# Stick-breaking sums on the scores' own PSUM bank, and attention scores over 64 partitions, in a two-block fp32 transformer kernel

## What is computed

```python
q = heads(proj[..., :MIX_WIDTH]); k = ...; v = ...
q = jnp.concatenate([partial_rope(q[:, :n_rot], pos), q[:, n_rot:]], axis=1)   # heads A and B turned
k = jnp.concatenate([partial_rope(k[:, :n_rot], pos), k[:, n_rot:]], axis=1)

def stick_breaking_attention(q, k, v):
    z = jnp.einsum('bhqd,bhkd->bhqk', q, k) * Dh ** -0.5
    log_1m = jnp.where(causal, jax.nn.log_sigmoid(-z), 0.0)          # causal is strict: key < query
    suffix = lax.cumsum(log_1m, axis=3, reverse=True) - log_1m
    a = jnp.where(causal, jnp.exp(jax.nn.log_sigmoid(z) + suffix), 0.0)
    return jnp.einsum('bhqk,bhkd->bhqd', a, v)
```

## Time and profile before

| | us |
|---|---|
| median of 3 runs | 2152.02 |
| lowest, highest | 2151.99, 2154.15 |
| the profiled execution | 2152.88 |
| its span in the profile | 2151.1 |

### The profile page before, as it was taken

One profiled execution on the slowest core, in us unless ns is written; L12 is line 12 of the kernel. 1 busy time (PEld: TensorE's weight loads), 2 busy tenths in 40 slices (PEclk: granted clock), 3 DMA queues, 4 the chain that ended last, 5 costly groups with the idle time before them and its releaser, 6 DMA issues.

```text
span 2151.1 us, 36602 instructions
## 1 busy us (share of the span) xinstructions
PE 2051.2 (95%) x15510; PEld 1966.5 (91%) x15510; DVE 930.2 (43%) x1761; ACT 917.4 (43%) x1393; POOL 1332.5 (62%) x612
## 2 busy tenths in 40 slices
PE   7999997999989999889999999999999999999998
PEld 4999996899989998769998999989999999988998
DVE  4554776561455477754124422144233432134223
ACT  2443454334444335434444354514544345514543
POOL 1778660477967786217887765505896765405885
PEclk8999998999989999999999999999999999999999
DMA  9997550785689775227555543335554543335552
GB/s 326 357 332 253 186 161 20 254 289 176 195 275 349 244 245 167 79 84 250 177 162 170 170 146 116 103 126 166 186 194 134 192 143 113 118 118 168 185 196 79
DMA packets 356787, 398.18 MB, mean 185 GB/s; under 512 B 8984, under 2 KB 318992, under 8 KB 356624
## 3 DMA queue, kind: packets, MB, share of 16 engines
q1 hardware_dynamic: 356464, 395.65, 55.5%
q10 hardware_dynamic: 160, 0.20, 0.0%
HBM read 394.77 MB, written 1.05 MB: 184 GB/s over the span
## 4 chain that ended last, share of the span: by engine, by line
PE 90%; DVE 5%; ACT 3%; SPq 1%; issue 1%; DMA 1%; DVEq 0%; ACTq 0%
PE bank L706 73%; PE bank L783 5%; PE bank L1108 3%; PE bank L938 1%; PE bank L805 1%; PE bank L900 1%; PE bank L1072 1%; SPq L534 1%; DVE arena L1641 1%; ACT arena L1270 1%; PE bank L697 1%; PE bank L999 1%; DVE arena L1685 1%; DMA arena<-in_ada_w 1%; PE bank L939 1%
## 5 line engine op out<-in xcount | busy, mean ns | idle before, releaser
L672 POOL TENSOR_TENSOR w_lo<-ring,w_hi 128x1024 fp32r<-128x1024 f32 (+2 forms) x608 | 1332.3, 2217 | 798.7 <-ACT w_hi L1169 798.1
L706 PE MATMUL bank<-hn,w_hi 128*128 128x256 f32 x2912 | 848.4, 291 | 26.4 <-DVE hn_lo L1578 15.8
L706 PE MATMUL bank<-hn_lo,w_hi 128*128 128x256 f32 x2912 | 832.4, 286 | 0.0
L706 PE MATMUL bank<-hn,w_lo 128*128 128x256 f32 x2912 | 832.1, 286 | 0.0
L1169 ACT ACTIVATE w_hi<-ring 128x1024 fp32r<-128x1024 f32 (+2 forms) x608 | 576.4, 975 | 485.6 <-PE bank L706 356.8
L706 PEld LDWEIGHTS bank<-hn,w_hi 128*128 128x128 f32 x2912 | 567.6, 195 | 36.7 <-issue 34.6
L706 PEld LDWEIGHTS bank<-hn_lo,w_hi 128*128 128x128 f32 x2912 | 567.8, 195 | 4.5 <-issue 3.8
L706 PEld LDWEIGHTS bank<-hn,w_lo 128*128 128x128 f32 x2912 | 567.3, 195 | 0.0
L706 PE MATMUL bank<-gated,w_hi 128*128 128x256 f32 x1408 | 249.7, 280 | 0.0
L706 PEld LDWEIGHTS bank<-gated,w_hi 128*128 128x128 f32 x1408 | 215.0, 187 | 0.0
L706 PE MATMUL bank<-gated,w_lo 128*128 128x256 f32 x704 | 196.4, 279 | 0.0
(11 more groups left out here) (188 smaller groups left out, 2130.1 us busy)
## 6 DMA issues: line engine op xcount, KB each, us to landing
ring<-in_ffn_w_in SPq DMA_DIRECT2D x88, 1024.0 KB, 6.1
ring<-in_w_in SPq DMA_DIRECT2D x72, 1024.0 KB, 5.1
arena<-in_ada_w SPq DMA_DIRECT2D x35, 2048.0 KB, 10.3
ring<-in_w_up SPq DMA_DIRECT2D x32, 1024.0 KB, 5.4
ring<-in_w_down SPq DMA_DIRECT2D x32, 1024.0 KB, 5.0
ring<-in_ffn_w_out SPq DMA_DIRECT2D x32, 768.0 KB, 4.4
ring<-in_ffn_w_out SPq DMA_DIRECT2D x32, 640.0 KB, 4.0
ring<-in_w_in SPq DMA_DIRECT2D x16, 512.0 KB, 3.6
```

The costliest lines, as they stand in the source:

```text
L672: pool.tensor_tensor(w_lo[:, q, ks], ring[:, r, k0:k0 + n], w_hi[:, q, ks], ALU.subtract) \
L706: last = mm(out, a, b, start=start and i == 0, stop=stop and i == 2)
```

## The change

1. `turned` of a stick head no longer computes the scores a second time. Its three products with sp accumulate onto the bank that `stick_scores` wrote, and that bank stays taken until ScalarE has copied it out (`copied`). Stick heads get four banks in turn (2, 3, 4, 5, kind "stick banks") instead of two and two.
2. `q2` has 12 pair tiles instead of 24 masked tiles. `scores` takes the 64 partitions of the head of both `q2` and `k2`, so that the score products of block two have 64 contraction rows: rows 0 to 63 for even heads, 64 to 127 for odd ones.
3. The rotary units of q and k go one way now: VectorE multiplies by cos and by the scale in one instruction, and no longer writes two masked copies for q; the half unit of k copies with a scale. ScalarE scales q as it copies out of the bank, and unit 5 is one ScalarE instruction instead of two.

```diff
--- before.py
+++ after.py
@@ -337,8 +337,8 @@
 def place_heads(heads):
 
-    n = {"two banks": 0, "four banks": 0, "tp": 0, "pb": 0, "ps": 0}
-    banks = {"two banks": (2, 3), "four banks": (2, 3, 0, 1), "pb": (4, 5)}
+    n = {"two banks": 0, "four banks": 0, "stick banks": 0, "tp": 0, "pb": 0, "ps": 0}
+    banks = {"two banks": (2, 3), "four banks": (2, 3, 0, 1), "stick banks": (2, 3, 4, 5), "pb": (4, 5)}
     last = {}
 
     def take(kind, size, frees):
@@ -354,9 +354,8 @@
     for u, h in enumerate(heads):
         h.u, h.pair = u, u // 2
         if h.kind == "stick":
-            h.sb = [take("two banks", 2, f"sp {h.name}")]
+            h.sb = [take("stick banks", 4, f"copied {h.name} 0")]
             h.tp = [take("tp", SLOTS, f"sp {h.name}"), take("tp", SLOTS, f"arg {h.name}")]
-            h.pb = [take("pb", 2, f"copied {h.name} 0")]
             h.ps = [take("ps", SLOTS, f"out {h.name}")]
         else:
             turned = 1 if h.kind == "diff" else len(h.maps)
@@ -452,7 +451,7 @@
         rows_n2 = view(8192 + 1536, P)
         rows_c = view(8192 + 1664, P)
 
-        q2 = view(0, 24, S)
+        q2 = view(0, 12, S)
         k2 = view(6144, 12, S)
         v2 = view(9216, 2, MIXW2)
         gates = view(12288, 24, S)
@@ -873,13 +872,13 @@
                     if of:
                         ada_reduce(*of)
 
-            def stick_scores(b, q, k, qi, ki, stop):
-
-
-                mm(b[:, 0:256], k[:, ki, 0:P], q[:, qi, :], start=True, stop=False)
-                mm(b[:, 256:384], k[:, ki, P:S], q[:, qi, P:S], start=False, stop=False)
+            def stick_scores(b, q, k):
+
+
+                mm(b[:, 0:256], k[:, 0:P], q, start=True, stop=False, skip_group_check=True)
+                mm(b[:, 256:384], k[:, P:S], q[:, P:S], start=False, stop=False, skip_group_check=True)
                 for c0 in (0, 256):
-                    last = mm(b[:, c0:c0 + P], ident_r[:], unseen[:], start=False, stop=stop and c0 > 0)
+                    last = mm(b[:, c0:c0 + P], ident_r[:], unseen[:], start=False, stop=c0 > 0, skip_group_check=True)
                 return last
 
             def scores(hd, q, k, maps=(0, 1)):
@@ -890,9 +889,15 @@
                     if free:
                         pe.wait_ge(done_by(free), eng.at(free))
                     b = bank[:, sbk]
+                    if hd.kind != "diff" and hd.kind != "fox":
+                        half = slice(64 * (qi % 2), 64 * (qi % 2) + 64)
+                        qh, kh = q[half, qi // 2], k[half, ki]
                     if hd.kind == "stick":
 
-                        last = stick_scores(b, q, k, qi, ki, True)
+                        last = stick_scores(b, qh, kh)
+                    elif hd.kind == "soft":
+                        mm(b[:, 0:P], qh[:, 0:P], kh[:, 0:P], start=True, stop=True)
+                        last = mm(b[:, P:SCW], qh[:, P:S], kh, start=True, stop=True)
                     else:
                         fox = hd.kind == "fox"
                         for c0, c1, n in ((0, P, P), (P, SCW, S)):
@@ -906,15 +911,11 @@
             def turned(hd, q, k, tile):
                 if hd.kind == "stick":
 
-                    (qi, ki, _, _), (pb, free) = hd.maps[0], hd.pb[0]
-                    if free:
-                        pe.wait_ge(done_by(free), eng.at(free))
-                    b, sp_ = bank[:, pb], tile[:, hd.tp[1][0], :]
-                    stick_scores(b, q, k, qi, ki, False)
+                    b, sp_ = bank[:, hd.sb[0][0]], tile[:, hd.tp[1][0], :]
                     pe.wait_ge(vector_done, eng.at(f"sp {hd.name}"))
-                    mm(b[:, 0:256], tab("neg_suffix"), sp_[:, 0:256], start=False, stop=False)
-                    mm(b[:, 128:256], tab("neg_ones"), sp_[:, 256:384], start=False, stop=False)
-                    mm(b[:, 256:384], tab("neg_suffix"), sp_[:, 256:384], start=False, stop=True) \
+                    mm(b[:, 0:256], tab("neg_suffix"), sp_[:, 0:256], start=False, stop=False, skip_group_check=True)
+                    mm(b[:, 128:256], tab("neg_ones"), sp_[:, 256:384], start=False, stop=False, skip_group_check=True)
+                    mm(b[:, 256:384], tab("neg_suffix"), sp_[:, 256:384], start=False, stop=True, skip_group_check=True) \
                         .then_inc(tensor_done, eng.step(f"arg {hd.name}"))
                     return
                 pe.wait_ge(vector_done, eng.at(f"scaled {hd.name}"))
@@ -1276,7 +1277,7 @@
                     act.wait_ge(tensor_done, eng.at(f"arg {hd.name}"))
                     if hd.ps[0][1]:
                         act.wait_ge(tensor_done, eng.at(hd.ps[0][1]))
-                    f(tt[:, hd.ps[0][0]], bank[:, hd.pb[0][0], 0:SCW], ACT.Exp) \
+                    f(tt[:, hd.ps[0][0]], bank[:, hd.sb[0][0], 0:SCW], ACT.Exp) \
                         .then_inc(scalar_done, eng.step(f"copied {hd.name} 0"))
                     return
                 for m in range(len(hd.pb)):
@@ -1409,13 +1410,12 @@
                     if i in ROTARY:
                         if p >= 2:
                             act.wait_ge(tensor_done, eng.at(f"rotary {ROTARY[p - 2]}"))
-                        f(raw[:, p % 2], b, ACT.Copy).then_inc(scalar_done, eng.step(f"z2 out {i}"))
+                        f(raw[:, p % 2], b, ACT.Identity, scale=0.125 if i < 6 else 1.0) \
+                            .then_inc(scalar_done, eng.step(f"z2 out {i}"))
                         return
                     b = b.rearrange("p (t s) -> p t s", t=2)
                     if i == 5:
-                        for a in range(2):
-                            f(q2[:, 4 * i:4 * i + 4, :].rearrange("p (t a) s -> p t a s", a=2)[:, :, a], b, ACT.Identity,
-                              scale=tab("in64_eighth", 1, a)).then_inc(scalar_done, eng.step(f"z2 out {i}" if a else None))
+                        f(q2[:, 10:12, :], b, ACT.Identity, scale=0.125).then_inc(scalar_done, eng.step(f"z2 out {i}"))
                         return
                     if i == 11:
                         dst = k2[:, 10:12, :]
@@ -1899,26 +1899,16 @@
                     rot = bank[:, 5 + n % 2].rearrange("p (c s) -> p c s", c=2)
                     half = i % 6 == 4
                     t = 1 if half else 2
-                    tt(by_cos[:, 0:t], src[:, 0:t], cosb[:, 0:t], ALU.mult) \
+                    dst, k0, scale = (q2, 2 * i, 0.125) if i < 6 else (k2, 2 * (i - 6), 1.0)
+                    stt(by_cos[:, 0:t], src[:, 0:t], scale, cosb[:, 0:t], ALU.mult, ALU.mult) \
                         .then_inc(vector_done, eng.step(None if half else f"by cos {i}"))
                     tt(rot[:, 0:t], rot[:, 0:t], sinb[:, 0:t], ALU.mult).then_inc(vector_done, eng.step())
+                    if half:
+                        ts(dst[:, k0 + 1, :], src[:, 1], scale, None, ALU.mult) \
+                            .then_inc(vector_done, eng.step(f"by cos {i}"))
                     dve.wait_ge(vector_done, eng.at())
-                    if i < 6:
-                        dst = q2[:, 4 * i:4 * i + 4, :].rearrange("p (t a) s -> p t a s", a=2)
-                        tt(rot[:, 0:t], rot[:, 0:t], by_cos[:, 0:t], ALU.add).then_inc(vector_done, eng.step())
-                        for m in range(2 if half else 0):
-                            ts(dst[:, 1, m], src[:, 1], tab("in64_eighth", 1, m), None, ALU.mult) \
-                                .then_inc(vector_done, eng.step(f"by cos {i}" if m else None))
-                        dve.wait_ge(vector_done, eng.at())
-                        for m in range(2):
-                            ts(dst[:, 0:t, m], rot[:, 0:t], tab("in64_eighth", 1, m), None, ALU.mult) \
-                                .then_inc(vector_done, eng.step(f"rotated {i}" if m else None))
-                    else:
-                        k0 = 2 * (i - 6)
-                        if half:
-                            dve.tensor_copy(k2[:, k0 + 1, :], src[:, 1]).then_inc(vector_done, eng.step(f"by cos {i}"))
-                        tt(k2[:, k0:k0 + t, :], rot[:, 0:t], by_cos[:, 0:t], ALU.add) \
-                            .then_inc(vector_done, eng.step(f"rotated {i}"))
+                    tt(dst[:, k0:k0 + t, :], rot[:, 0:t], by_cos[:, 0:t], ALU.add) \
+                        .then_inc(vector_done, eng.step(f"rotated {i}"))
                     dve.wait_ge(vector_done, eng.at())
                 attention(HEADS_TWO, tile2, lambda hd: o2[:, hd.out_tile, :], lambda i: None)
                 for i in range(4):
```

## The result

Over nine runs of each, the kernel after takes 2157.02 us (2156.12 to 2158.99) where the kernel before takes 2152.21 us (2151.27 to 2154.15). The ratio is 1.0022, with an interval of 1.0012 to 1.0032. So it is slower by 4.8 us; the forecast was 0.2 us less, and the result lies 0.02 us above the upper end of the range. The profiled execution after took 2156.4 us, with a span of 2154.5 against 2151.1 before.

The account below looks back on a forecast made before the run. TensorE, busy for 95% of the span, was taken to bound the kernel. Part 1's -10.4 and part 2's +10.2 us, with nothing for part 3, gave -0.2: 2151.8 us from 2152.02, range 2146.0 to 2157.0.

Parts of the forecast that it names:

- What bounds the kernel: Whole kernel: TensorE, busy for 95% of the span; in block two only the softmax heads leave it slack, 4.0 us.
- Part 1, 10.4 us: Stick heads: dropping the second `stick_scores` at 12 places on the path gains 0.87 us each, bounds 9.8 and 10.7.
- Part 2, 10.2 us: Score products of block two over 64 rows: a loss of 68 changes of row count at 0.15 us each.
- the term for one change, 0.15 us: TensorE, between products of 128 and 64 rows: each change of row count costs 0.15 us, bounds 0.10 and 0.20.
- its upper bound: At each change of row count: 0.20 us if the next product waits 0.11 for its load, 13.6 us in all.
- The count, 80 - 12: Score groups of both layers: 80 changes, 2 lost in a wait at the start, 10 in softmax-head waits; 68 remain.
- free: Rival at the score groups: changes of row count cost nothing, only the 10.4 us gain stays, 2141.6 us; chance 0.13.
- half paid: Rival at the score groups: only the way in or the way out costs, 5.1 - 10.4 = -5.3, 2146.7 us; chance 0.08.
- cost 0.27: Rival: load behind each change begins only at the product's recorded end, 0.27 us each, +8.0, 2160.0 us; chance 0.10.
- Part 3, nothing: Rotary units: savings on VectorE (13.0 us of masked writes) and edits on ScalarE change nothing, since TensorE covers them.
- every bound on one side: Whole kernel, slow side: 78 changes at 0.20 with the low gain, 15.6 - 9.8 = +5.8, 2157.8 us.

## Why the prediction was wrong

**What bounds the kernel**: right. The stretches stayed full, and 15.1 us less of VectorE changed nothing.

**Part 1, 10.4 us**: right in kind and nearly in size. Alone it measured 9.86 under the heads, since the filler in two steps of each layer got 0.18 longer. In the kernel after these fillers are as short as before. No wait for a bank, for sp or for a copy came up: `L1280`, the copy, has the 491 ns of the earlier trace rows, and TensorE is full from 1354 to 1405 us.

**Part 2, 10.2 us**: the step that failed is the term for one change, 0.15 us. The moment of the load was read rightly from the transposes, 0.08 ahead of the recorded end. What followed was not: "the product after it can start 0.06 later" rested on two loads 0.06 apart at the change from 62 to 40 rows, a pair without a change between them. Measured are 0.20 in the chain at every change, 0.194 in b0 to b5, 0.193 with the second scores kept. That is the working with the other number: 0.28 - 0.08 + 0.11 - 0.12 = 0.19, as if the product waited for a whole load. The prediction had named this as its upper bound ("if the product after a change had to wait 0.11 for its load and not 0.06", 0.20) and chosen against it. For layer 0, 34 x 0.195 = 6.6 against 6 x 0.87 = 5.2 is +1.4, and +1.32 were measured.

**The count, 80 - 12**: right, and shown by the three kinds of heads apart: 10 of 16, 12 of 12, 12 of 12. The rivals did not come true: the changes are not free (2141.6 would have needed that, and is near what part 1 alone gives, 2143.3), not half paid (0.63 and 0.37 in the chain are the way in and the way out), and they do not cost 0.27, since the load does begin before the recorded end.

**Part 3, nothing**: right, by the kernel with part 3 left out, to 0.01 us per stage. The product by cos with three operands takes as long as the one with two, and VectorE's wait for TensorE took up the rest; the group of after against L1902 in the earlier trace rows:

```profile
L1903 DVE SCALAR_TENSOR_TENSOR arena<-bank,const 128x512 f32<-128x512 f32 (+1 forms) x20 | 12.8, 638 | 100.7 <-PE bank L1073 100.7
```

**What was missing**: the clock. By the stages of the profiled executions, of the 5.0 us between -0.2, the forecast difference, and the 4.8 measured, 68 x 0.045 = 3.1 belong to the size of a change, 1.2 to the half clock in layer 1 and 0.8 to the norm stages. The latter two could not be read from the trace of before, but the norm stages in it differ by 2.0 us between the layers (190.01 and 188.01), and a bound of that size on either side would have been due. The range was also narrower than its own working: with every bound on one side the prediction had 2157.8, and it ended the range at 2157.0. The loss itself is clear of the noise (0.12 to 0.32%), in two sets of runs.

The Trainium skill (TensorEngine Tiling (Array Packing), section Key Properties) has the rule that changing the tiling mode drains TensorE. The trace agrees, in both directions and at 128 to 256 columns: the load waits until 0.07 to 0.08 us before the recorded end of the last product, and 0.20 us are lost. The page has no price; here it is 68 x 0.195 = 13.3 us, more than leaving out twelve score computations brings.

## What to carry to other kernels

Halving the contraction rows of a product saves nothing on TensorE, and where its neighbours use all 128 rows each change of row count costs about 0.2 us of a full stream, on the way in and on the way out: count the changes, not the products. Score products that follow each other with 64 rows pay for one change in and one out (L879 behind L878 pays nothing), so if 64 rows must be, putting them together should help; no run here tried a longer row of them. Zeros in a masked tile are the cheaper way to select a head if the other engines have the slack to write them. Two edits that come together should be priced, and run, apart: the first alone makes this kernel 0.4% faster, and the second takes back more than that.

## What the runs showed of the hardware

- At a change between 128 and 64 rows the weight load starts 0.07 to 0.08 us before the recorded end of the product before it, where in a stream of 128 rows it started 0.27 before, and TensorE loses 0.20 us in the chain, whichever way the change goes and whichever half of the rows is used (even and odd heads show the same 0.63 and 0.37).
- In all five profiles in which the eight score products of a2 had 64 rows, TensorE fell to 1.2 GHz for 3.4 us behind its wait of 1.43 us, in layer 1 and not in layer 0; in the five with 128 rows it did not. It cost 1.2 us. Whether the rows or the moment of arrival decide is not shown.
- After one and the same idle stretch of 3.1 us in the norm, the half clock lasted 0, 3.4 or 6.8 us, worth 0, 0.8 or 1.9 us. A kernel that arrives some microseconds earlier or later can win or lose that for no other reason; the lead of the kernel with 64 rows in b0 to b5 over that with c0 to c5, 1.5 us, is of this kind.
